# The four sums of the value weights per contraction tile: made on GpSimd right behind their loads, instead of on VectorE between its splits

## The reference

```python
if layer == N_A_LAYERS - 1:
    k_sb, v_sb = jnp.split(rms_norm(h, kv_norm) @ w_kv, 2, axis=-1)
```

## Time and profile before

| | |
|---|---|
| median of 3 runs | 1471.95 us (1471.65 to 1474.85) |
| profiled execution, span | 1470.1 us (the profile gives no time of that execution beside its span) |
| TensorE busy | 1461.1 us, 99% |
| VectorE busy | 998.4 us, 68% |
| ScalarE busy | 716.7 us, 49% |
| GpSimd busy | 122.7 us, 8% |
| DMA, mean | 244 GB/s |
| granted TensorE clock, mean | 0.999 |

### The profile page before, as it was taken

One profiled execution on the slowest core, in us unless ns is written; L12 is line 12 of the kernel. 1 busy time (PEld: TensorE's weight loads), 2 busy tenths in 40 slices (PEclk: granted clock), 3 DMA queues, 4 the chain that ended last, 5 costly groups with the idle time before them and its releaser, 6 DMA issues.

```text
span 1470.1 us, 18207 instructions
## 1 busy us (share of the span) xinstructions
PE 1461.1 (99%) x6842; PEld 1221.1 (83%) x6842; DVE 998.4 (68%) x1317; ACT 716.7 (49%) x1066; POOL 122.7 (8%) x184
## 2 busy tenths in 40 slices
PE   9999999999999999999999999999999999999998
PEld 7888888888888888888888888888888888888886
DVE  6775568465576896856578676566566556678987
ACT  6764544444544545763325654433333423455465
POOL 0001111111110000000010001110111111100000
PEclk9999999999999999999999999999999999999999
DMA  9877778786796887477999866677887777879853
GB/s 339 292 286 221 162 196 248 172 244 147 196 262 171 323 321 263 152 263 274 324 374 355 295 221 221 228 224 178 241 242 207 223 203 214 250 220 330 314 200 144
DMA packets 154189, 357.97 MB, mean 244 GB/s; under 512 B 7824, under 2 KB 23440, under 8 KB 150032
## 3 DMA queue, kind: packets, MB, share of 16 engines
q1 hardware_dynamic: 103824, 205.98, 39.9%
q0 software_dynamic: 29376, 102.77, 28.3%
q10 hardware_dynamic: 20928, 48.41, 9.0%
HBM read 310.99 MB, written 113.25 MB: 289 GB/s over the span
## 4 chain that ended last, share of the span: by engine, by line
PE 99%; DMA 1%; SPq 0%; ACT 0%; issue 0%; DVE 0%; ACTq 0%
PE main L2126 24%; PE main L2125 24%; PE main L2124 24%; PE aux L2126 5%; PE aux L2124 5%; PE aux L2125 5%; PE aux L2486 2%; PE aux L2432 2%; PE aux L2428 2%; PE aux L2430 2%; PE main L2432 1%; PE main L2428 1%; PE main L2430 1%; PE aux L2475 1%; DMA w_raw<-in_w_mem_kv 1%; PE aux L2268 0%
## 5 line engine op out<-in xcount | busy, mean ns | idle before, releaser
L2124 PE MATMUL main<-act_hi,w_hi 128*128 128x512 f32 x1216 | 475.5, 391 | 0.0
L2126 PE MATMUL main<-act_hi,w_lo 128*128 128x512 f32 x1216 | 473.8, 390 | 0.0
L2125 PE MATMUL main<-act_lo,w_hi 128*128 128x512 f32 x1216 | 473.6, 389 | 0.0
L2126 PEld LDWEIGHTS main<-act_hi,w_lo 128*128 128x128 f32 x1216 | 228.3, 188 | 47.9
L2125 PEld LDWEIGHTS main<-act_lo,w_hi 128*128 128x128 f32 x1216 | 228.4, 188 | 46.8
L2124 PEld LDWEIGHTS main<-act_hi,w_hi 128*128 128x128 f32 x1216 | 228.4, 188 | 46.4
L1332 DVE SCALAR_TENSOR_TENSOR w_lo<-w_raw,gains,w_hi 128x512 fp32r<-128x512 f32 x180 | 123.3, 747 | 120.8 <-ACT w_hi L702 120.8
L702 ACT ACTIVATE w_hi<-w_raw,gains 128x512 fp32r<-128x512 f32 x180 | 115.4, 712 | 140.9 <-PE main L2126 121.8
L1323 DVE TENSOR_TENSOR w_lo<-w_raw,w_hi 128x1024 fp32r<-128x1024 f32 x88 | 104.2, 1222 | 94.0 <-ACT w_hi L695 93.8
L695 ACT ACTIVATE w_hi<-w_raw 128x1024 fp32r<-128x1024 f32 x88 | 88.5, 1057 | 153.0 <-PE main L2126 109.5
L2124 PE MATMUL main<-w_hi,act_hi 128*128 128x512 f32 x336 | 131.0, 390 | 0.0
(11 more groups left out here) (333 smaller groups left out, 2082.6 us busy)
## 6 DMA issues: line engine op xcount, KB each, us to landing
w_raw<-in_w_in_a SPq DMA_DIRECT2D x32, 1024.0 KB, 7.7
w_raw<-in_w_in_b SPq DMA_DIRECT2D x32, 1024.0 KB, 7.5
weight_sums<-in_w_out_a POOLq DMA_DIRECT2D x48, 512.0 KB, 7.1
weight_sums<-in_w_out_b POOLq DMA_DIRECT2D x48, 512.0 KB, 7.5
weight_sums<-weight_sums POOLq DMA_DIRECT2D x32, 512.0 KB, 7.0
w_raw<-weight_sums SPq DMA_DIRECT2D x16, 1024.0 KB, 8.0
work<-weight_sums SPq DMA_DIRECT2D x16, 1024.0 KB, 7.6
w_raw<-in_w_mem_kv SPq DMA_DIRECT2D x13, 1024.0 KB, 5.2
```

The source lines that it names most:

```text
L2124: TE.matmul(o, a[0], b[0], start=first, stop=False)
L2125: TE.matmul(o, a[0], b[1], start=False, stop=False)
L2126: return TE.matmul(o, a[1], b[0], start=False, stop=final)
```

## The change

`weight_sums` is moved from VectorE's program into GpSimd's. There it is called ahead of `store_sums(step)` for each of the eight steps, with the same waits and the same four additions. `SUM_SLABS` and the three places that called it on VectorE are gone.

```diff
-SUM_SLABS = (3, 4, 6, 7, 9, 10)
...
+            def weight_sums(n):
+
+                pool.wait_ge(ts_loaded[n % 2], 32 * (n // 2) + 32)
+                b11, b12, b21, b22 = (wide[n % 2][:, m, :] for m in range(4))
+                nc.gpsimd.tensor_tensor(b11, b11, b12, ALU.add).then_inc(ts_made, 1)
+                nc.gpsimd.tensor_tensor(b12, b12, b22, ALU.add).then_inc(ts_made, 1)
+                pool.wait_ge(ts_made, 4 * n + 1)
+                nc.gpsimd.tensor_tensor(b22, b11, b22, ALU.add).then_inc(ts_made, 1)
+                pool.wait_ge(ts_made, 4 * n + 3)
+                nc.gpsimd.tensor_tensor(b21, b22, b21, ALU.add).then_inc(ts_made, 1)
+
...
                     for step in range(KQ):
+                        weight_sums(step)
                         store_sums(step)
...
-            def weight_sums(n):
-
-                dve.wait_ge(ts_loaded[n % 2], 32 * (n // 2) + 32)
-                b11, b12, b21, b22 = (wide[n % 2][:, m, :] for m in range(4))
-                V.tensor_tensor(b11, b11, b12, ALU.add).then_inc(ts_made, 1)
-                V.tensor_tensor(b12, b12, b22, ALU.add).then_inc(ts_made, 1)
-                dve.wait_ge(ts_made, 4 * n + 1)
-                V.tensor_tensor(b22, b11, b22, ALU.add).then_inc(ts_made, 1)
-                dve.wait_ge(ts_made, 4 * n + 3)
-                V.tensor_tensor(b21, b22, b21, ALU.add).then_inc(ts_made, 1)
...
-                if i in SUM_SLABS:
-                    weight_sums(SUM_SLABS.index(i))
...
-                if n == 7:
-                    weight_sums(6)
...
-                if n == 12:
-                    weight_sums(7)
```

## The result

The kernel after takes 1482.49 us (median of 4 runs, 1482.22 to 1484.24) against 1471.91 before, a ratio of 1.0073 with a 95% interval of 1.0061 to 1.0084. I had said 1492 in a range of 1478 to 1510, slower with a chance of 0.88.

What follows compares the result with a forecast made beforehand. TensorE, busy 1461.1 of 1470.1 us, was taken as the bound. The span 1470.1 + 18.4 (wait before tile 14) + 2.1 (clock) gave 1490.6; with 1.85 for the median of runs, 1492.5, rounded to 1492; range 1478 to 1510.

Steps and rivals of the forecast that it cites:

- The bound and what VectorE's relief is worth: TensorE alone sets the end; taking 30.5 us of additions off VectorE gives nothing back.
- The price of an addition: On GpSimd, a 128x768 addition with two inputs takes 1.85 us, bounded by 0.954 and 2.4.
- the hindrance of GpSimd: GpSimd's additions meeting VectorE's work by chance: half an instruction, 0.61 us, at some of 28 additions, 7.6 us in all.
- The sum for step 6's landing: GpSimd's rounds of sums + 12.73 us make step 6's store land at 812.7; TensorE waits 18.4 us before tile 14.
- The limit itself: Step 6's store landing later than 794.3 makes TensorE wait before tile 14, microsecond for microsecond.
- Exclusion: Each GpSimd addition waits 1.22 us for VectorE; step 6 lands at 839, TensorE waits 45 us, about 1520; chance 0.12.
- its other half: VectorE's splits are held likewise, by 1.85 us each time; held to be hidden in the key slabs.
- In time after all: Step 6's store lands before 794.3 if additions take under 1.46 us each; 1472, no change; chance 0.10.
- The clock: TensorE's value tiles after its wait: one tile's worth, 2.1 us, between nothing and 4.2.
- What would make it wrong: Additions under 1.5 us, TensorE waiting first before another tile, or SyncE's wait adding more than a microsecond or two.
- the forecast of 20.5 us: Added to the span: TensorE's wait before tile 14, 18.4 us, and a lower clock after it, 2.1 us.

Runs made afterwards that it cites:

- the gaps: All sums on GpSimd, each addition waiting for the one before it, against the kernel before: 1483.95 us, ratio 1.0089.
- the store made late: Kernel before with 28 memsets on GpSimd ahead of step 6's store, against the kernel before: 1478.60 us, ratio 1.0041.
- beside memsets: Kernel before with 14 memsets of a scratch tile on GpSimd ahead of step 6's store, against the kernel before: 1471.47 us, ratio 0.9997.
- GpSimd copies with one input: Kernel before with 9 scratch-tile copies on GpSimd ahead of step 6's store, against the kernel before: 1471.85 us, ratio 1.0000.
- 12.4 us of additions: Kernel before with 6 idle scratch-tile additions on GpSimd ahead of step 6's store, against the kernel before: 1475.26 us, ratio 1.0020.

## Why the prediction was right, and where its steps were wrong

- **The bound and what VectorE's relief is worth.** Right. Additions taken from VectorE gave TensorE nothing: the two kernels with 24 and 28 of them on GpSimd take 1471.6, as long as the kernel before.
- **The price of an addition.** Right: unhindered 1.83 to 1.87 us against 1.85 worked out from select and memset. The estimate by the page GPSIMD Engine Reference of the Trainium skill, section Elementwise — side-by-side cycle accounting, 1.69, was 9% low. The first sum began at 665.99 (666.5 forecast). With all hindrance the 32 additions took 2.03 us on average, 1.85 + 0.18; I had 0.27 for the hindrance of GpSimd.
- **The sum for step 6's landing, the first step that failed.** I took 10.4 and 11.13 us for a landing from the kernel before. The six waits came down to 7.1 us each, and with them the rounds to 17 us instead of 21; the last landing took 5.6. Six times 4.0 and once 4.8 are 29 of the 30.5 us between 812.7 and 782.2. In the kernel before, a store often stands directly behind the two loads on GpSimd's queue: at 696.78 and 756.23 less than 0.1 us behind, with waits of 12.5 and 11.1 us for them; at 783.44 no load is near and the landing takes 8.8. After the change four additions lie between the loads and the store. The other kernels agree with this: in the three that have this order in the first six steps (the change, the gaps, the first six steps on GpSimd) the six waits are 39.0 to 42.7 us in all, and in the seven in which VectorE makes these sums, 63.4 to 66.8. But no run moved a store away from the loads and left the rest alone, and it isn't all: step 6's store has no load directly ahead in either kernel and still took 8.8 us before and 5.6 after. Why is open. The limit itself was right, as the store made late shows; the change never came near it.
- **Exclusion, and whom it hits: the step that the 10.6 us come from.** I gave this rival 0.12 and let it act on the ring: GpSimd waits for VectorE, the store is late. What happened is its other half, in the same paragraph: VectorE's splits are held. I priced that at one addition, 1.85 us, and dismissed it for the key slabs, which was right (24 additions there are free), and forgot the value stage, where the margins that I had read myself are 1 us. The hold was up to 5.5 us at a time, three additions, and late low parts cost TensorE 8.5 us, the clock behind them 3.9. The page SBUF — State Buffer of the Trainium skill, section Who interferes with whom, names the pairs correctly: an input in PSUM escapes the hold (677 to 693 ns throughout), a GpSimd instruction that only writes does not hold (945 to 959 ns beside memsets). But its lock for one instruction lets one expect a wait of one addition, and the trace has three in step 6, one at a time in step 7.
- **"In time after all".** The store was in time, by 12 us, and the time was not 1472 all the same. My condition for it, 1.46 us an addition, used the same wrong landings.
- **The clock.** I took one tile, 2.1 us, between 0 and 4.2. In the profiled execution it cost 3.9 in two stretches, in the late-store run some 2.
- **What would make it wrong** named this case: that TensorE waits first before another tile, late splits instead of a late store. By that the account was wrong, although 1482.5 lies in the range. That the forecast of 20.5 us and the 10.6 measured fall into one range is chance: one wait that did not exist against another that had not been priced.

## What to carry to other kernels

Work moved from VectorE to GpSimd can stay on VectorE's path as long as VectorE's own instructions read two tiles of SBUF and the moved ones read SBUF too: here the addition is twice as long on GpSimd, and its whole length can be taken from VectorE. Ask for each place how far ahead of its consumer VectorE is; additions that end ahead of the tight stretch were free here, four in it cost 5.7 us. A landing time is read under one order of loads and stores; here it did not hold under another (7.1 us a wait instead of 11.1).

## What was not expected of the hardware

- A VectorE instruction with two SBUF inputs was held over three successive GpSimd additions (6.77 us instead of 1.22) and got in ahead of the fourth, the one for which GpSimd waits for its last result. It isn't always so: the same program alternates one for one in step 7 of the change, and with the last two steps alone on GpSimd it alternates in step 6 and holds for three additions in step 7 (6.11 us instead of 0.95 for one low part). What decides between the two is open. With a wait before every addition they alternate throughout, at no gain in time.
- The hold is recorded as duration, on both engines: VectorE's busy time rose by 6.8 us although 30.5 us of work had gone.
- GpSimd copies with one input hold VectorE too, but less: 2.3 us in 11.9 us of copies, against 5.6 in 12.4 us of additions. Why a copy holds for only a part of its time stays open.
